# The final norm of block one and the first norm of block two as one factor per token, applied behind the projection and the gates

## The reference, cut to what matters

```python
    x = x + _conv_ffn(h, ff_w_up[i], ff_conv_w[i], ff_conv_b[i], ff_w_down[i])   # block 1, last layer
    return _rmsnorm(x, final_norm_g)
...
    h = rmsnorm(x, norm_mix_pre[l])                                              # block 2
    (c_q, c_kv, k_r, sg_u, sg_v, cv_x, cv_b, cv_c, pool_in, gate_pre) = split_cols(h @ w_in[l])
    gates = jax.nn.sigmoid(gate_pre + gate_b[l]).reshape(B_, S_, N_BRANCH, D_)
...
    x = x + rmsnorm(merged @ w_out[l], norm_mix_post[l])
```

## Time and profile before

| | |
|---|---|
| median of the runs | 3323.23 us (3321.57 to 3323.7, three runs) |
| span of the profiled execution, first to last instruction | 3301.4 us |
| median of the runs less that span | 21.8 us |
| TensorE, matmul | 3137.2 us busy, 95% |
| VectorE | 1574.7 us, 48% |
| GpSimd | 1192.8 us, 36% |
| ScalarE | 1105.8 us, 33% |
| chain that ended last | TensorE 75%, issue 10%, VectorE 7%, GpSimd 4%, ScalarE 3% |
| mean granted TensorE clock | 0.977 of full |

### The profile page before, as it was taken

One profiled execution on the slowest core, in us unless ns is written; L12 is line 12 of the kernel. 1 busy time (PEld: TensorE's weight loads), 2 busy tenths in 40 slices (PEclk: granted clock), 3 DMA queues, 4 the chain that ended last, 5 costly groups with the idle time before them and its releaser, 6 DMA issues.

```text
span 3301.4 us, 62854 instructions
## 1 busy us (share of the span) xinstructions
PE 3137.2 (95%) x25712; PEld 2394.2 (73%) x25712; DVE 1574.7 (48%) x2299; ACT 1105.8 (33%) x1559; POOL 1192.8 (36%) x617
## 2 busy tenths in 40 slices
PE   7999999979899899999999999989999899899999
PEld 5757888848688886877777866448888665448887
DVE  6755554085255555677321520536061577745160
ACT  5413443212434333443234313232222334522221
POOL 3332444414143331444443423014444256214443
PEclk9999999989899999999999999999999799999999
DMA  3212223313100001455423322113322122022333
GB/s 132 83 45 77 96 95 101 103 57 96 33 3 3 3 3 54 164 183 186 153 90 99 96 77 83 33 57 96 96 95 96 51 70 85 1 70 95 97 98 99
DMA packets 74610, 268.61 MB, mean 81 GB/s; under 512 B 8719, under 2 KB 8730, under 8 KB 74240
## 3 DMA queue, kind: packets, MB, share of 16 engines
q1 hardware_dynamic: 73536, 262.53, 24.5%
q0 software_dynamic: 896, 3.52, 0.3%
HBM read 261.71 MB, written 2.10 MB: 80 GB/s over the span
## 4 chain that ended last, share of the span: by engine, by line
PE 75%; issue 10%; DVE 7%; POOL 4%; ACT 3%; DMA 0%; POOLq 0%; DVEq 0%; ACTq 0%; SPq 0%
PE gp L388 54%; POOL w_low L357 4%; PE gp L1227 4%; PE gp L2194 2%; PE gp L314 2%; PE gp L2818 2%; PE aux L1357 1%; PE aux L1227 1%; PE gp L2702 1%; DVE arena L1679 1%; DVE aux L3056 1%; PE aux L1222 1%; PE aux L2650 1%; ACT arena L667 0%; PE aux L746 0%
## 5 line engine op out<-in xcount | busy, mean ns | idle before, releaser
L357 POOL TENSOR_TENSOR w_low<-ring,w_high 128x1024 fp32r<-128x1024 f32 x397 | 956.8, 2411 | 1711.8 <-ACT w_high L326 1711.8
L326 ACT ACTIVATE w_high<-ring 128x1024 fp32r<-128x1024 f32 x397 | 420.1, 1059 | 1326.6 <-PE gp L388 1271.6
L388 PE MATMUL gp<-ffn_h,w_high 128*128 128x512 f32 x2432 | 757.2, 393 | 12.9 <-DVE ffn_h L418 5.1
L388 PEld LDWEIGHTS gp<-ffn_h,w_high 128*128 128x128 f32 x2432 | 454.8, 188 | 123.4 <-POOL w_low L357 12.6
L388 PE MATMUL gp<-ffn_h,w_low 128*128 128x512 f32 x1216 | 474.6, 390 | 0.0
L388 PE MATMUL gp<-ffn_high,w_high 128*128 128x512 f32 x928 | 362.0, 390 | 3.3 <-POOL w_low L357 3.2
L388 PE MATMUL gp<-ffn_low,w_high 128*128 128x512 f32 x864 | 336.6, 390 | 0.0
L388 PE MATMUL gp<-ffn_high,w_low 128*128 128x512 f32 x864 | 336.6, 390 | 0.0
L388 PEld LDWEIGHTS gp<-ffn_h,w_low 128*128 128x128 f32 x1216 | 229.3, 189 | 48.4
L2116 DVE TENSOR_TENSOR arena<-arena 128x512 f32<-128x512 f32 x64 | 152.9, 2389 | 200.2 <-ACTq L163 200.2
L388 PE MATMUL gp<-in_h,w_high 128*128 128x512 f32 x768 | 240.3, 394 | 4.5 <-DVE in_h L416 4.5
(11 more groups left out here) (496 smaller groups left out, 5011.0 us busy)
## 6 DMA issues: line engine op xcount, KB each, us to landing
ring<-in_weights SPq DMA_DIRECT2D x437, 512.0 KB, 3.5
H<-in_ada SPq DMA_DIRECT2D x48, 512.0 KB, 4.2
arena<-arena SPq DMA_DIRECT2D x32, 67.5 KB, 2.0
X<-in_x SPq DMA_DIRECT2D x4, 512.0 KB, 8.1
out_x<-X SPq DMA_DIRECT2D x8, 256.0 KB, 3.8
arena<-in_sm POOLq DMA_DIRECT2D x1, 1024.0 KB, 5.0
cst<-in_cst SPq DMA_DIRECT2D x1, 756.0 KB, 9.9
arena<-in_hy_f_w POOLq DMA_DIRECT2D x1, 512.0 KB, 5.3
```

Source lines behind the costliest of these rows:

```text
L326: nc.scalar.activation(w_high[:, slab % PARTS, :], ring[:, slab % RING, :], ACT.Copy).then_inc(high_ready, 1)
L357: nc.gpsimd.tensor_tensor(w_low[:, slab % PARTS, :], ring[:, slab % RING, :], w_high[:, slab % PARTS, :], ALU.subtract).then_inc(low_ready, 1)
L388: last = nc.tensor.matmul(gp[:, t.bank, :], wt[:, slab % PARTS, w], x(k), start=(k == 0 and q == 0), stop=(k == sum(kt) - 1 and q == 2))
```

## The change

The functions `final1_*` go. In `down1` of the second layer, X stays unnormed. ScalarE makes the high part of X times the product of both gains, a square of X and a square of X times the first gain; VectorE makes the low part and adds up both kinds of squares, one tile behind the residual. The product of the gains is one instruction of 128 x 8 at the start of `down1`, for which ScalarE waits. TensorE sums both squares between the first and second tile of `in2`. ScalarE and VectorE make a common factor of them (`COMB`), in four steps of Ln and Exp and two products or sums, and VectorE multiplies each of the 48 results of `in2`, `gate2a` and `gate2b` in PSUM by it before ScalarE reads it. X itself gets its first norm on VectorE beside tiles 2 to 5 of `in2`. VectorE's side work is cut up and put between the scalings, the small loads wait for the end of `down1`, and arena tiles change places.

The diff, cut to its core (the three functions that are only cut into steps are left out):

```diff
-        _, bH = in_arena(("gap3", 16), ("in2_h", 2 * DT))
+        _, bH = in_arena(("gap3", 48), ("in2_h", 2 * DT))
...
-            squares_beside_act(act, a, f"down{layer}", Xk, arena_tiles(ffX2), x_wait(act, n_act))
+            if layer:
+                final_gain_act(act, a)
+            else:
+                squares_beside_act(act, a, f"down{layer}", Xk, arena_tiles(ffX2), x_wait(act, n_act))
...
-            residual_dve(dve, v, f"down{layer}", sq=arena_tiles(ffX2), beside=(lambda j: ada_dve(dve, v, 2 * F1T + j) if j < MODS - 2 * F1T else None) if layer else None)
+            if layer:
+                final_gain_dve(dve, v, lambda j: ada_dve(dve, v, 2 * F1T + j) if j < MODS - 2 * F1T else None)
+            else:
+                residual_dve(dve, v, f"down{layer}", sq=arena_tiles(ffX2))
...
-        def final1_pe(pe):
-            folded_norm_pe(pe, arena_tiles(ffX2))
-
-        def final1_act(act, a):
-            root_norm_act(act, a)
-
-        def final1_dve(dve, v):
-            norm_dve(dve, v, DT, Xk, lambda k: pcol("final_norm", k), Xk, x_ready)
+        LN_1, INV_1, LN_2, ROOT_1 = (H[:, i, :] for i in range(4))
+        final_sums, final_ln, final_scaled, in2_scaled = rw_mean, rw_bsum, rw_bon, rw_gn
+        PAST = DT
+
+        def final_gain_act(act, a):
+
+            base = n_act.x - DT
+
+            def made(k):
+                act.wait_ge(x_ready, base + k + 1)
+                split_gain_act(k, "norm_mix_pre2", 0, tiles_of(bH))
+                nc.scalar.activation(sq_x(k), X[:, k, :], ACT.Square).then_inc(sq_ready, 1)
+                nc.scalar.activation(sq_g(k), X[:, k, :], ACT.Square, scale=pcol("final_norm", k)).then_inc(sq_ready, 1)
+
+            n_act.x += DT
+            for t in loop_tiles(act, STAGE["down1"], a):
+                if t.j == 0:
+                    act.wait_ge(final_scaled, PAST + 1)
+                else:
+                    made(t.j - 1)
+                split_ahead_act(act, t)
+            made(DT - 1)
+
+        def final_gain_dve(dve, v, beside):
+
+            gains = lambda name: par[:, POFF[name]:POFF[name] + DT]
+            v.go(nc.vector.tensor_tensor(gains("norm_mix_pre2"), gains("norm_mix_pre2"), gains("final_norm"), ALU.mult))
+            v.tell(final_scaled)
+
+            def made(k):
+                dve.wait_ge(sq_ready, n_dve.sq + 2 * k + 2)
+                split_gain_dve(k, "norm_mix_pre2", 0, tiles_of(bH), tiles_of(bH, DT))
+                if k:
+                    v.go(nc.vector.tensor_tensor(sq_x(k), sq_x(k), sq_x(k - 1), ALU.add))
+                    v(nc.vector.tensor_tensor(sq_g(k), sq_g(k), sq_g(k - 1), ALU.add))
+
+            for t in loop_tiles(dve, STAGE["down1"], v):
+                consume_wait(dve, t)
+                x = X[:, t.j, :]
+                v.go(nc.vector.tensor_tensor(x, gp[:, t.bank, :], x, ALU.add))
+                v.tell(drained[t.bank], x_ready)
+                if t.j:
+                    made(t.j - 1)
+                beside(t.j)
+            made(DT - 1)
+            v.tell(sq_folded)
             n_dve.x += DT
+            n_dve.h += DT
+            n_dve.sq += 2 * DT
+
+        def final_sums_pe(pe):
+
+            n_pe.folds += 1
+            n_pe.sq += 2 * DT
+            pe.wait_ge(sq_folded, n_pe.folds)
+            nc.tensor.matmul(aux[:, 0, :], ones, sq_x(DT - 1), start=True, stop=True)
+            nc.tensor.matmul(aux[:, 1, :], ones, sq_g(DT - 1), start=True, stop=True).then_inc(final_sums, 1)
+
+        def final_roots_act(act, a):
+
+            nc.scalar.preload_act_table_set("natural_log_exp_and_others")
+            act.wait_ge(final_sums, PAST + 1)
+            a(nc.scalar.activation(LN_1, aux[:, 0, :], ACT.Ln, scale=1.0 / D, bias=const("eps")))
+            nc.scalar.activation(INV_1, LN_1, ACT.Exp, scale=-1.0).then_inc(final_ln, 1)
+            nc.scalar.activation(ROOT_1, LN_1, ACT.Exp, scale=-0.5).then_inc(final_ln, 1)
+            act.wait_ge(final_scaled, PAST + 2)
+            nc.scalar.activation(LN_2, INV_1, ACT.Ln, scale=1.0 / D, bias=const("eps")).then_inc(final_ln, 1)
+            act.wait_ge(final_scaled, PAST + 3)
+            nc.scalar.activation(COMB, LN_2, ACT.Exp, scale=-0.5).then_inc(final_ln, 1)
+            n_act.x += DT
+
+        def final_roots_dve(dve, v):
+
+            dve.wait_ge(final_ln, PAST + 1)
+            v.go(nc.vector.tensor_tensor(INV_1, INV_1, aux[:, 1, :], ALU.mult))
+            v.tell(final_scaled)
+            dve.wait_ge(final_ln, PAST + 3)
+            v.go(nc.vector.tensor_tensor(LN_2, LN_2, LN_1, ALU.add))
+            v.tell(final_scaled)
+            dve.wait_ge(final_ln, PAST + 4)
+
+        def final_norm_dve(dve, v, lo, hi):
+
+            for k in range(lo, hi):
+                nc.vector.scalar_tensor_tensor(out=X[:, k, :], in0=X[:, k, :], scalar=pcol("final_norm", k), in1=ROOT_1,
+                                               op0=ALU.mult, op1=ALU.mult).then_inc(x_ready, 1)
+                n_dve.x += 1
+
+        def in2_scale(dve, v, t):
+
+            consume_wait(dve, t)
+            z = gp[:, t.bank, :]
+            nc.vector.tensor_tensor(z, z, COMB, ALU.mult).then_inc(in2_scaled, 1)
...
-        bCQ, bCKV, bKR, bU, bV, bCX, bCB, bCC, bP, bQ, bG, bOUT = 0, 2, 3, 4, 6, 8, 10, 12, 14, 16, 32, 48
-        sm = arena[:, 56:61, :].rearrange("p a b -> p (a b)")
+        bCQ, bCKV, bKR, bU, bV, bCX, bCB, bCC, bP, bQ, bG, bOUT = 0, 2, 3, 4, 6, 8, 10, 12, 14, 48, 32, 16
+        sm = arena[:, 24:29, :].rearrange("p a b -> p (a b)")
...
-        POS = arena[:, 61, :]
-        RCNT = arena[:, 62:64, :]
+        POS = arena[:, 29, :]
+        RCNT = arena[:, 30:32, :]
...
-            pool.wait_ge(h_ready, 5 * DT)
+            pool.wait_ge(slab_done, STAGE["in2"].slab0)
...
-            norm_pe(pe, DT, Hk)
             def beside(j):
+                if j == 1:
+                    final_sums_pe(pe)
...
         def two_act(act, a):
-            pre_norm_act(act, a)
-            high_act(act, a, tiles_of(bH))
             for t in loop_tiles(act, STAGE["in2"], a, body=16):
                 split_ahead_act(act, t)
-                consume_wait(act, t)
+                if t.j == 0:
+                    final_roots_act(act, a)
+                act.wait_ge(in2_scaled, PAST + t.j + 1)
...
                 for t in loop_tiles(act, STAGE[name], a, body=16):
                     split_ahead_act(act, t)
-                    consume_wait(act, t)
+                    act.wait_ge(in2_scaled, PAST + (32 if free else 16) + t.j + 1)
                     if free:
                         act.wait_ge(merged, t.j + 1)
                     a.go(nc.scalar.activation(arena[:, bG + t.j, :], gp[:, t.bank, :], ACT.Sigmoid,
...
-        def trig_dve(v):
+        def trig_dve(v, step):
...
         def two_dve(dve, v):
-            split_norm_dve(dve, v, "norm_mix_pre2", bH)
...
-            dve.wait_ge(sm_in, 16 * 4)
...
-            for i in range(2):
+
...
+            for t in loop_tiles(dve, STAGE["in2"], v, body=16):
+                if t.j == 0:
+                    final_roots_dve(dve, v)
+                in2_scale(dve, v, t)
+                if t.j in (2, 3, 4, 5):
+                    final_norm_dve(dve, v, 2 * t.j - 4, 2 * t.j - 2)
+                if t.j == 7:
+                    latent(2, bCQ, "q_norm2")
+                if t.j == 9:
+                    latent(1, bCKV, "kv_norm2")
+                if t.j == 11:
+                    centre_dve(dve, v, 2, arena_tiles(bV))
+                if t.j == 14:
+                    scale_shift_dve(dve, v, 2, arena_tiles(bV), lambda k: pcol("sg_ln_g2", k), lambda k: pcol("sg_ln_b2", k),
+                                    arena_tiles(bV), ln_ready)
+
+            def spatial_weights():
+                dve.wait_ge(sm_in, 16 * 4)
+                for g in range(4):
...
+                v.tell(sgw_ready)
...
+            for t in loop_tiles(dve, STAGE["gate2a"], v, body=16):
+                if t.j == 0:
+                    dve.wait_ge(in2_ready, 16)
+                    spatial_weights()
+                in2_scale(dve, v, t)
+                if t.j in (0, 1):
+                    short_conv(t.j)
+                if t.j in (2, 3):
+                    pool_level(0, t.j - 2)
+                if 4 <= t.j < 8:
+                    pool_level(1, t.j - 4)
+                if 8 <= t.j < 12:
+                    trig_dve(v, t.j - 8)
...
                 v.tell(sg_out)
+            for t in loop_tiles(dve, STAGE["gate2b"], v, body=16):
+                in2_scale(dve, v, t)
             dve.wait_ge(trig_done, 2)
...
             (ffn1_pe, ffn1_act, ffn1_dve, None, (0,)),
             (rwkv_pe, rwkv_act, rwkv_dve, rwkv_pool, ()),
             (ffn1_pe, ffn1_act, ffn1_dve, None, (1,)),
-            (final1_pe, final1_act, final1_dve, None, ()),
             (two_pe, two_act, two_dve, two_pool, ()),
```

(32 more changed lines are left out.)

45 lines of the change are left out of this document (21 added, 24 removed).

## The result

| | before | changed |
|---|---|---|
| median | 3321.64 us (five runs, 3321.09 to 3323.7) | 3303.68 us (five runs, 3298.09 to 3307.41) |
| span of the profiled execution | 3301.4 us | 3301.9 us |
| mean granted clock of that execution | 0.977 | 0.974 |

The ratio is 0.9948 (95% interval 0.9934 to 0.9961): faster by over 0.2%, and the median of 3303.7 lies on the low end of the range. But the two profiled spans are the same, and the changed kernel's time is its span plus 1.8 us, not plus 21.8.

The account below looks back on a forecast made before the run. TensorE, busy for 95% of the span, was taken as the bound. 19.1 - 2.15 - 0.6 - 0.7 - 0.9 = 14.75 us, 14.6 kept, gave span 3286.8 and time 3308.6 us; range 3303.7 to 3312.5.

Parts of the forecast that it names:

- The seam: From `down1` to `in2`: both roots leave TensorE's way, so `in2`'s second tile is done 19.1 us sooner.
- part 7: Last of X's eight parts, in `in2`'s first tile: ready 1.35 us after TensorE wants it.
- rival (a): VectorE and GpSimd don't meet at the seam: 3306.5 us, or 3303.7 if `down1`'s wait is hidden too; chance 0.13.
- The factor's chain: Behind `in2`'s second tile: common factor and first scaling end at 1731.6, next slab split 0.6 us late within 1.6 slack.
- First: Start of `down1`: ScalarE waits for the product of the two gains, its slab split starts 2.15 us later.
- second: Second tile of `down1`: a low part ahead of the modulation's accumulation delays SyncE's load and the slabs, 0.7 us.
- third: End of `gate2b`: a scaling and a hop come before ScalarE's last gate, 0.9 us.
- The clock's part of the first: `down1`'s start: the longer stop keeps TensorE at half clock longer, 0.6 us more, bounds 0 and 1.2.
- (c): `in2` starts some 20 us earlier and meets weights that have not landed: 16 us lost, 3324.6 us; chance 0.05.
- (d): VectorE's side work becomes the pace of `gate2a`: 28 us less 1.6 slack lost, 3335 us; chance 0.03.
- Rival (b): Two small seam stops drop TensorE to 1.2 GHz: 1.35 us lost, 3310.0 us, or 3310.6 with `down1`'s full 1.2; chance 0.2.
- 21.8 us lie around the span and stay: Whole kernel: median 3323.2 less profiled span 3301.4 was taken as constant time outside the span, added to span 3286.8.

Follow-up runs that it names:

- a1: The changed kernel, unchanged, run once more: 3301.3 us, ratio 0.9945.
- gatelast: Changed kernel, but the last tile of `gate2b` is not multiplied by the common factor: this execution took 3288.3 us.
- slack: Changed kernel with four more exponentials on ScalarE inside the common factor's chain: the execution took 3298.2 us.
- adafirst: Changed kernel, but in `down1` VectorE makes the modulation's accumulation ahead of the low part of the tile before: the execution took 3305.4 us.
- a0: The changed kernel, unchanged, run again: 3297.1 us, ratio 0.9943.
- early: Changed kernel, but the product of the two gains is made at the start of `up1`, not of `down1`: 3298.1 us, ratio 0.9943.
- Experiments 3, 4 and 5: Changed kernel with, one each: gains' product at `up1`'s start (3298.1 and 3298.6 us); accumulation before low part (3305.4); `gate2b`'s last tile unscaled (3288.3).
- b1: The kernel before, unchanged, once more: a long execution, 3318.0 us.
- b0: The kernel before, unchanged, run again: median 3313.5 us, ratio 0.9988 to the same kernel's other 17 runs.
- all3: Changed kernel with gains' product at `up1`'s start, accumulation before low part in `down1`, and last two tiles' low parts before their folds: 3295.3 us, ratio 0.9932.
- earlylow: Changed kernel with gains' product at `up1`'s start and the last two tiles' low parts ahead of their folds: 3299.1 us, ratio 0.9932.
- early1: Changed kernel with gains' product at `up1`'s start, the same edit run once more: 3298.6 us, ratio 0.9930.

## Why the prediction was right, and where it wasn't

**The seam.** 19.1 us was forecast, and the ruler shows 19.1 in each of the five profiles of the changed kernel or a variant that had no half-clock stretch there (changed, a1, gatelast, slack, adafirst); with one of 3.4 us it is 17.4 (a0 and the early ones). The terms: 1.31 us for part 7 (forecast 1.35), 0.33 for the folds (0.7), 1.42 of TensorE for the sums (1.72), the second tile done 14.8 us after the split at 1726.93, where the forecast has 14.8 behind 1716.87. That the totals agree to 0.1 us is in part luck: these three terms came out 0.7 us smaller, and the products around them 0.75 us slower (5.88 us without the stop for the first tile's, 5.87 for the second's, where the forecast has 5.53 and 5.46). What sets the forecast apart from rival (a) is the exclusion of VectorE and GpSimd, and it held: 2.90 beside 0.68 us. So (a) is out, although its second number, 3303.7, is the median measured.

**The factor's chain** with the first scaling ended at 1741.4, 14.5 us after the split at 1726.93 (forecast 14.7), the split behind it 0.54 us late (0.6), without a stop. Slack: 1.6 forecast with 0.6 used, about 0.9 found left. The table load was 1.28 us, as the rows before had it. The 2.7 that the Trainium skill counts ("ScalarE: Activation LUTs", section "Table sets: the hidden batching unit") are, by the section "What ACT_TABLE_LOAD costs" of the same page, a load of about 1283 ns and a drain of about 1380; the trace agrees with the first and has no drain: the load starts 0.02 us behind the split's end, and Ln 0.02 us behind the load's. The load ended at 1736.31, just as the sums did (ScalarE's Ln follows at 1736.33), so a load of 2.7 us would have put the chain 1.4 us later, past the 0.9 left: the rows' figure mattered, if only by 0.5 us.

**The added waits.** First 2.05 us (forecast 2.15) and with the clock 2.7 to 3.35 (2.75); second 0.76 (0.7), ruler 0.43 to 0.72; third 0.74 (0.9). Experiments 3, 4 and 5 undid them one by one. The clock's part of the first is 0.7 to 1.3 us, where the forecast has 0.6 with bounds 0 and 1.2. It was also read a little wrong: the earlier trace rows give 2.9 and 5.0 us at half clock and not 2.7 and 5.1, so half of the difference is 0.5. GpSimd's loads, `gate2a` and the slabs: nothing, the ruler shows 0.00 from the third tile of `in2` to the end of `gate2a` and again over the branches with `gate2b`, in every profile of the changed kernel itself. Rivals (c) and (d) are out.

**Rival (b)**, the clock, was too narrow. At the seam it came true in some executions (1.7 us), but what it left out is larger: the stretch in the attention (+1.2 in changed and a1, none in a0; in b1, without the change, +1.8), and falls in code that the change never touches.

**The step that failed** is "21.8 us lie around the span and stay". 1.8 us lie around a span in every run. The profiled execution of before was simply a short one, 3301.4 us of span where the usual one of this kernel has about 3318, and I set its span beside the median of other executions and called the difference overhead. The net of the edited stages, forecast 14.6, came out at 13.1 to 13.5 (the attention's clock is in it). Taken from the short execution that would be 3290, from the median 3310. The medians lie 18 to 21 us apart, the means of the 57 and the 17 executions 16: 10.1 in span times clock, and 6.1 because the clock took less from the changed kernel, 92 us on average in before, 86 in it (span less span times clock). The 13 us of the stages, which hold their own clock, are most of this. By the profiles, the other 3 us come from falls elsewhere. So that 3303.7 lies within the range is in part luck with the clock. Why the changed kernel's executions meet fewer long falls isn't settled; both kernels have executions with and without the one in block three.

## What to carry to other kernels

Where roots stand between two matmul stages, most of the gain is in not waiting for them: here 13.5 us for having the products ahead of the factor, and 5.6 for the merged chain, the input parts made early and the passes over X left out, all together. Before setting an estimate against a median, ask whether the profiled execution is a typical one: compare its span and its granted clock with those of several runs, and compare kernels stage by stage with a ruler of like instructions, because 10 us of clock can hide 4 us of work. Where a wait is taken away, look along the whole trace for what moved with it: here the four profiles that save 2 us of stop lose 4.8 to 6.4 us to the clock 300 us later, by a way that no run shows.

## What the runs showed of the hardware that I had not expected

One program on one core takes 3302 to 3330 us, and the mean granted clock (0.977 to 0.970) goes with it almost one to one. The falls looked at here sit where TensorE does small matmuls or stops, but whether one lasts 3.4 or 17 us isn't the program's doing alone. Behind the first branch the fall came in four of four profiles of kernels in which one small VectorE instruction stands at the start of `up1`, some 250 us earlier than in the changed kernel, and in none of seven without. After the same stop of 2.7 to 2.8 us at `down1`'s start the clock stood at half for 3.4 us in before, b0, b1, all3 and earlylow, and not at all in early and early1. Every table load on ScalarE, in the profiles of before and of the changed kernel, took 1.28 us, and where the next instruction was ready it followed 0.01 to 0.02 us later.
